# Weighted values of two attention groups: the bank summed by one VectorE reduction, the halves of v kept apart until the output projection

## The reference, cut to what matters

```python
weights = jnp.where(mask, jnp.exp(log_beta + later), 0.0)
return jnp.einsum('bhqk,bhkd->bhqd', weights.astype(v.dtype), v)
...
merged = jnp.concatenate([rmsnorm(merge_heads(o_sb), sb_out_norm),
                          rmsnorm(merge_heads(o_dl), dil_out_norm)], axis=-1)
return merged @ w_out
```

## Time and profile before

| | us |
|---|---|
| median of 3 runs (2080.09 to 2082.62) | 2080.28 |
| profiled execution | 2083.61 |
| its span | 2081.8 |

### The profile page before, as it was taken

How to read it: one execution, slowest core, us unless ns; L and a number is a source line. 1 busy time by engine, 2 the same in 40 slices (tenths; PEclk the granted TensorE clock), 3 DMA queues, 4 the chain that set the end, 5 groups by cost and what they waited for, 6 DMA issues and landing times. The chain is left out here.

```text
span 2081.8 us, 25977 instructions
## 1 busy us (share of the span) xinstructions
PE 1932.0 (93%) x9224; PEld 1582.6 (76%) x9224; DVE 1257.5 (60%) x1649; ACT 908.3 (44%) x1467; POOL 753.1 (36%) x506
## 2 busy tenths in 40 slices
PE   5899999999999898989989976896999999999998
PEld 4788888888888676767767755685788888888886
DVE  6855556555556266676676677327856556554555
ACT  6433333333335455555555555306433333333334
POOL 2656656530000252242242335304656556540000
PEclk9999999999999999999999986897999999999999
DMA  3443544558664310010101112511534435458663
GB/s 143 153 166 131 193 151 144 190 192 290 195 192 144 116 46 26 21 56 25 51 25 40 31 36 70 193 41 71 186 143 160 174 132 185 152 203 308 192 192 142
DMA packets 95584, 276.01 MB, mean 133 GB/s; under 512 B 10480, under 2 KB 14704, under 8 KB 89840
## 3 DMA queue, kind: packets, MB, share of 16 engines
q1 hardware_dynamic: 95472, 274.59, 38.7%
HBM read 190.14 MB, written 80.22 MB: 130 GB/s over the span
## 5 line engine op out<-in xcount | busy, mean ns | idle before, releaser
L703 PE MATMUL banks<-ffn_x_operands_hi 128*128 128x512 f32 x616 | 239.8, 389 | 0.0
L706 PE MATMUL banks<-ffn_x_operands_hi,ffn_x_operands_lo 128*128 128x512 f32 x616 | 239.7, 389 | 0.0
L705 PE MATMUL banks<-ffn_x_operands_lo,ffn_x_operands_hi 128*128 128x512 f32 x616 | 239.6, 389 | 0.0
L1265 DVE TENSOR_TENSOR heads_wt<-banks,heads_wt 128x512 fp32r<-128x512 f32 (+1 forms) x160 | 100.9, 632 | 134.7 <-ACT heads_wt L1109 133.9
L1382 PE MATMUL banks<-first_hi,w_hi 128*128 128x512 f32 x384 | 161.1, 420 | 13.5 <-ACT heads_qk_raw L1131 7.9
L401 ACT ACTIVATE scaled_rows<-banks 128x512 f32<-128x512 f32 x132 | 78.6, 595 | 201.9 <-PE banks L690 201.9
L516 DVE TENSOR_TENSOR scaled_rows<-banks,scaled_rows 128x512 f32<-128x512 f32 x132 | 91.1, 690 | 118.1 <-PE banks L690 74.4
L986 POOL TENSOR_TENSOR scaled_rows<-scaled_rows,heads_stay 128x128 f32<-128x128 f32 (+7 forms) x64 | 86.1, 1351 | 210.9 <-DVE heads_stay L1225 210.9
L1384 PE MATMUL banks<-first_hi,w_lo 128*128 128x512 f32 x384 | 152.2, 396 | 0.0
L1383 PE MATMUL banks<-first_lo,w_hi 128*128 128x512 f32 x384 | 152.0, 396 | 0.0
L687 PE MATMUL banks<-first_hi,ffn_w_ring_hi 128*128 128x512 f32 x352 | 139.1, 395 | 11.8 <-DVE first_lo L567 11.8
(11 more groups left out here) (183 smaller groups left out, 4821.0 us busy)
## 6 DMA issues: line engine op xcount, KB each, us to landing
w_raw<-in_ffn_w_gate SPq DMA_DIRECT2D x22, 1024.0 KB, 6.8
ffn_up_raw<-in_ffn_w_up SPq DMA_DIRECT2D x22, 1024.0 KB, 6.1
ffn_down_raw<-in_ffn_w_down SPq DMA_DIRECT2D x22, 1024.0 KB, 4.9
down_operands<-ffn_down_raw SPq DMA_DIRECT2D x22, 1024.0 KB, 7.3
w_raw<-h_operands SPq DMA_DIRECT2D x52, 256.0 KB, 3.0
ffn_up_raw<-h_operands SPq DMA_DIRECT2D x52, 256.0 KB, 3.0
ffn_down_raw<-h_operands SPq DMA_DIRECT2D x50, 256.0 KB, 3.0
w_raw<-in_w_in SPq DMA_DIRECT2D x24, 512.0 KB, 4.0
```

What stands on the lines that cost most here:

```text
L703: pe.matmul(out, hi[:, 0, tok], hi[:, 1, :], start=(opens and c == 0), stop=False, skip_group_check=True)
L705: pe.matmul(out, hi[:, 0, tok], lo[:, 1, :], start=False, stop=False, skip_group_check=True)
L706: last = pe.matmul(out, lo[:, 0, tok], hi[:, 1, :], start=False, stop=(c == NP - 1), skip_group_check=True)
L1265: dve.tensor_tensor(wt[:, wt_slot(s, j), 0:tiles, 1, :], b.ps[:, bank, 0:tiles * P].rearrange("p (t c) -> p t c", c=P), wt[:, wt_slot(s, j ...
```

## The change

ScalarE's copy and both VectorE adds are replaced by one VectorE reduction over the hi and lo columns of the bank, on all 128 partitions. `o_stage` and `o_dram` hold the two halves (products of v hi, products of v lo) apart. The wait of VectorE is now for `pv_ready`, TensorE's own. In the output block each piece is loaded as two, GpSimd adds them to `o_sum` (two tiles of `w_raw` and two new ones), ahead of each fold by two pieces; hi is taken from the first half, lo is the sum minus hi, and the squares are of the sum. The product of both lo parts is now part of the result.

```diff
-        o_stage = sb("o_stage", [HEAD, 2, SEQ])
+        o_stage = sb("o_stage", [P, 2, SEQ])
-        o_low = sb("o_low", [HEAD, 2, P])
...
             def store_part(it, kind, part):
                 cols = slice(part * HALF, (part + 1) * HALF)
                 sp.wait_ge(o_copied, 1 + STEPS * run(it, kind) + 4 * part + 4)
-                for head in range(2):
-                    first = address(sp, kind * GROUP + it * P + head * HEAD)
-                    sp.dma_start(o_dram[bass.ds(first, HEAD), cols], o_stage[:, head, cols]
-                                 ).then_inc(o_stored[part], 16)
+                first = address(sp, kind * GROUP + it * P)
+                for v_part in range(2):
+                    sp.dma_start(o_dram[v_part, bass.ds(first, P), cols].rearrange("(h r) c -> r h c", r=HEAD),
+                                 o_stage[v_part * HEAD:(v_part + 1) * HEAD, :, cols]).then_inc(o_stored[part], 16)
...
-            def values_low(it, kind, s):
-
-                act.wait_ge(pv_ready, 4 + BANKS * run(it, kind) + bank_count(s + 1))
-                act.activation(o_low[:, :, :], values[HEAD:P, :, 0, :], ACT.Copy
-                               ).then_inc(o_low_done, 1)
...
                     weights_hi(it, kind, s, j, project)
-                    if values_done(it, kind, s, j):
-                        values_low(*values_done(it, kind, s, j))
...
-                n = STEPS * run(it, kind) + s + 1
-                dve.wait_ge(o_low_done, n)
-                dve.tensor_tensor(o_low[:, :, :], values[0:HEAD, :, 1, :], o_low[:, :, :], ALU.add
-                                  ).then_inc(o_low_sum, 1)
-                dve.wait_ge(o_low_sum, n)
-                dve.tensor_tensor(o_stage[:, :, s * P:(s + 1) * P], values[0:HEAD, :, 0, :], o_low[:, :, :], ALU.add
-                                  ).then_inc(o_copied, 1)
+                dve.wait_ge(pv_ready, 4 + BANKS * run(it, kind) + bank_count(s + 1))
+                dve.tensor_reduce(o_stage[:, :, s * P:(s + 1) * P], values.rearrange("p a n c -> p a c n"),
+                                  mybir.AxisListType.X, ALU.add).then_inc(o_copied, 1)
...
+        o_more = sb("o_more", [P, 2, D])
+        o_sum = [part.rearrange("p (f c) -> p f c", c=OQ) for part in (
+            b.w_raw[:, 0, :, :].rearrange("p k f -> p (k f)"), b.w_raw[:, 1, :, :].rearrange("p k f -> p (k f)"),
+            o_more[:, 0, :], o_more[:, 1, :])]
...
-                    sp.dma_start(o_raw[n % 4], o_dram[group * GROUP:(group + 1) * GROUP, q * OQ:(q + 1) * OQ]
-                                 .rearrange("(f p) c -> p f c", p=P)).then_inc(o_loaded[n % 4], 16)
+                    for v_part, to in enumerate((o_raw, o_sum)):
+                        sp.dma_start(to[n % 4], o_dram[v_part, group * GROUP:(group + 1) * GROUP,
+                                                       q * OQ:(q + 1) * OQ]
+                                     .rearrange("(f p) c -> p f c", p=P)).then_inc(o_loaded[n % 4], 16)
...
+            def both_parts(n):
+                pool.wait_ge(o_loaded[n % 4], 32 * (n // 4 + 1))
+                pool.tensor_tensor(o_sum[n % 4], o_raw[n % 4], o_sum[n % 4], ALU.add).then_inc(o_added, 1)
+
+            for n in range(2):
+                both_parts(n)
             for n in range(2 * QUARTERS):
-
+                if n + 2 < 2 * QUARTERS:
+                    both_parts(n + 2)
                 first = n % 2 * (KT // 2)
                 pool.wait_ge(o_squared, n + 1)
...
-                    act.wait_ge(o_loaded[n % 4], 16 * (q // 2 + 1))
+                    act.wait_ge(o_loaded[n % 4], 32 * (q // 2 + 1))
...
-                    act.activation(o_sq[:, features(group), :], o_raw[n % 4], ACT.Square).then_inc(o_squared, 1)
+                    act.wait_ge(o_added, n + 1)
+                    act.activation(o_sq[:, features(group), :], o_sum[n % 4], ACT.Square).then_inc(o_squared, 1)
...
                     dve.wait_ge(o_hi_done, n + 1)
-                    dve.tensor_tensor(o_lo[:, features(group), tok], o_raw[n % 4],
+                    dve.wait_ge(o_added, n + 1)
+                    dve.tensor_tensor(o_lo[:, features(group), tok], o_sum[n % 4],
...
-    o_dram = nc.dram_tensor("o_between", [D, SEQ], F32, kind="Internal").ap()
+    o_dram = nc.dram_tensor("o_between", [2, D, SEQ], F32, kind="Internal").ap()
```

More of the change, by code:

```diff
@@ L863, in heads_block @@
         out_w_hi_done, out_w_gained, out_w_split = (sem(f"out_w_{n}") for n in ("hi_done", "gained", "split"))
-        pv_ready, o_low_done, o_low_sum, o_copied = (
-            sem("pv_ready"), sem("o_low_done"), sem("o_low_sum"), sem("o_copied"))
+        pv_ready, o_copied = sem("pv_ready"), sem("o_copied")
         o_stored = [sem(f"o_stored{h}") for h in range(2)]
@@ L1188, in step @@
                     split_out_weights(s)
-                if last and s == STEPS - 1:
-                    values_low(it, kind, s)
             def one_run(it, kind, first=0, end=STEPS, project=True, last=False):
@@ L1549, in output_block @@
         x_loaded = [sem(f"out_x_loaded{t}") for t in range(TT // 2)]
-        o_hi_done, o_split, o_squared = sem("out_o_hi_done"), sem("out_o_split"), sem("out_o_squared")
+        o_added, o_hi_done, o_split, o_squared = sem("out_o_added"), sem("out_o_hi_done"), sem("out_o_split"), sem("out_o_squared")
         o_halved, o_folded, stored = sem("out_o_halved"), sem("out_o_folded"), sem("out_x_stored")
```

## The result

The changed kernel took 2092.84 us in the median of 4 runs (2092.66 to 2094.54), beside 2081.28 us (2080.09 to 2082.62, 4 runs) for the kernel before on the same chip: a ratio of 1.0052, with a 95% interval of 1.004 to 1.0064. Between the medians it is slower by 11.6 us in the first set and by 9.4 in the second; the forecast was 2082.1, with a range up to 2091.

A forecast was written before the change was run, and what follows sets the result against it. TensorE was taken as the bound, busy 1932.0 of 2081.8 us, so only its waits count. Heads -7.8, stores 0, output block +9.6 gave +1.8 us on the 2080.28 median: 2082.1 us, range 2074 to 2091.

The forecast's parts named there:

- The signs: What would show the forecast: reduction near 0.69 us, copy-out waits 4 to 5 us smaller, heads about 8 us shorter.
- The first step, 26 waits x 0.17: Heads: TensorE's 26 waits for the copy out of the values' bank each end 0.17 us earlier, 4.4 us.
- the sum of the three, 7.8 us of waits: Heads: 4.4 us from named waits, 2.2 from half the other 27, 1.2 in the last run; 7.8 us less.
- third rival: Heads: shorter waits save a third of the lost clock, 6.3 us, on top; 2075.8 us; chance 0.19.
- 9.6 forecast: Output block: the fifth bank starts 9.6 us later, through later loads and GpSimd's adds and folds before the sums.
- From there TensorE is full, so the 9.6 us stay: Output block behind the second sums: TensorE is full, so the 9.6 us delay stays.
- GpSimd's chain to the second sums ends later still and hides that: Output block: a slower clock after the 5 us stall doubles the third bank's 2.7 us, but GpSimd's chain hides it.
- The adds at 2.0 us: Output block: each GpSimd add of the two halves takes 2.0 us.
- Stores at zero, up to +1: Heads' end: only the last, larger store counts; taken as zero, with ends -0.4 and +1 us.
- the 0.6 us "earlier": Heads' end: the last store starts 0.6 us earlier through the lost ScalarE copy and the 0.17, offsetting its later landing.
- The first rival: Output block loses 13 us with adds at 2.4 us, heads gain only 4.4; 2088.9 us; chance 0.26.
- its smaller gain in the heads: First rival's heads: only the 26 named waits shorten, 4.4 us.

The follow-up runs named there:

- the second: Later set timing the same changed kernel again, against the kernel before: 2091.46 us, ratio 1.0046 (1.0032 to 1.006).
- without adds: Changed kernel with double loads but GpSimd's adds left out, hi, lo and squares from the first half: 2078.37 us, 0.9984 to the kernel before.
- Heads alone: Changed heads with the kernel before's output block, which reads only the first half: 2075.28 us, 0.9965 to the kernel before.
- the two kernels built on it: Changed heads, old output block: with ScalarE's copy put back, 2075.67 us; with one reduction for each head instead of one for both, 2080.44 us.
- adds behind folds: Changed kernel with GpSimd's queue reordered, both folds of a quarter before the next adds: 2084.61 us, 1.001 to the kernel before.
- with the adds on VectorE: Changed kernel with the adds of the halves moved from GpSimd's queue to VectorE's: 2081.04 us, 0.9992 to the kernel before.
- with x loaded later: Changed kernel with the adds on VectorE and the first load of x issued behind both groups' loads: 2082.46 us, 0.9998 to the kernel before.

## Why the prediction was wrong

**Where it held.** The reduction took 0.68 us (forecast 0.69); the place in the queue 0.60. Here the rule of the Trainium skill ("VectorE: DVE Perf Modes") can be judged: by its section on the perf-mode tier table a reduction runs at the single rate, and the trace agrees, since 512 numbers take as long as in the two-input subtraction (680 and 686 ns). The advice of its Rules for kernel authors, to restructure a reduction as the slowest op, isn't borne out where two dependent adds are what it replaces. The heads won 7.5 us (forecast 7.8), the copy 1 to 2 of them (forecast 1.2). TensorE's first matmul came 2.95 us later (forecast 2.6), and it stood before both sums, for the folds, in the order worked out. Mechanism and sign of both parts were right.

**Where the heads were right by luck.** The signs asked for TensorE's waits for the copy out 4 to 5 us smaller; they are 2 to 3 us smaller (33.6 to 33.7 in three profiles of the old one, 30.4 to 31.9 in seven of the new). The first step, 26 waits x 0.17, was too large, and so was the sum of the three, 7.8 us of waits: TensorE's idle time fell by about 3 us in all. That a shortened step ends at the next wait would explain it, and is not shown. The other 4.4 us are busy time, at a higher granted clock. That is the third rival's mechanism, with less than its 6.3 us and not on top of the forecast. That shorter waits raised the clock is the reading of two numbers side by side; no run here separates it.

**Where it failed: the terms of the output block**, 9.6 forecast and 14.9 us in this profile. The path was right; its pieces were sized too small, and the clock and the store were put at nothing. By the table of marks, in the order of their size in this profile:

- *"From there TensorE is full, so the 9.6 us stay"*: 1.7 us more came behind the second sums. TensorE was full, but not fast: the clock fell at 1333.86, after the 1.9 us stall. With the folds first, or without adds, that stretch took 80.8 us as before.
- *"GpSimd's chain to the second sums ends later still and hides that"*: it doesn't, 1.4 us. The chain begins with ScalarE's root of the first sums, and the sums themselves ran at the lower clock, 1.86 us instead of 0.95. So the squares came 3.96 us after the sums' start where I had taken 3.04 from the row before, and everything behind them is later by 0.9; the rest is the add (2.35 us until the fold behind it, for 2.0) and some 0.2 us before and in the fold ahead of it. Cover can't be claimed for a chain that starts from the slowed instruction.
- *The adds at 2.0 us*: 2.35 to 2.40 us. One stands ahead of the first lo part. Up to the first sums only the third and the fourth count in the queue, as the earlier ones wait for loads. Together with a third load that landed 9.5 us after the first instead of 8.7, fold 1 ended 18.3 us after the first landing; 17.1 had been worked out. That is 1.2 us, 0.35 of them before the first matmul. In the other two profiles of this block the third load came 10.8 and 10.9 us after the first, and this term is the largest of the four, at 2.5 us and more. Part of it was in the rows: the earlier trace rows give one landing for the fifth and the sixth load, 1319, but the sixth landed at 1319.9, which makes 3.1 us a MB instead of 2.9.
- *Stores at zero, up to +1*: 0.97 us, at the upper end. The two stores land 3.2 us after issue instead of 2.3, and the 0.6 us "earlier" that I set against it is not found here: measured from the end of the last copy out, it lies in the heads' gain, and I had set it against the stores as well. Heads alone and the two kernels built on it show the same within 0.02 us.

0.97 + 1.2 + 1.4 + 1.7 = 5.3 us, and 9.6 + 5.3 = 14.9. With the heads at -8.8 that makes +6.1 us; the other 2.6 us of this profile lie in blocks that the change doesn't touch. Against the medians one more thing counts: the profiled execution of before was itself 3.3 us above the 2080.28 from which the forecast was counted (2.3 above the median of all four runs), that of after at its median.

**The range.** The first rival was nearest: adds at 2.4 us, 13 us lost in the output block, 2088.9 us. Its price for the block was 2 us short of this profile, for the clock and the store, where it shared the forecast's terms (worked through again with its own 2.4 and 2.6 us, the block's loss is 12.4 us rather than 13), and its smaller gain in the heads didn't come. The range reached 2091 by its adds and the smaller gain. The ends of terms that I had named myself are 3.4 us for the adds, 1 for the store, and the slower clock, which I had put at nothing and which cost 2.6 (0.9 ahead of the second sums, 1.7 behind them): all of them raise the same stage, and came together. With them in one sum the block alone leads to 2082.1 + 7.0 = 2089.1 us, and the smaller gain in the heads on top, 3.4, to 2092.5. The measured 2092.84 lies just above even that.

## What to carry to other kernels

Taking work off the chain of one stage by handing its remainder to the next is a price paid where the next stage starts cold: there nothing hides an operation. Before an in-order queue gets a new instruction that waits for a transfer, list what stands behind it; here the order alone was worth 8 us and the choice of engine 10 to 12, more than the whole gain that was sought. When a stall on TensorE is forecast, add the slower clock to everything that starts from TensorE's next instruction, and once more after the next stall. A term that hangs on queued loads is better taken from several profiles: here one landing, against the first, moved by 1.4 us between profiles of the same block.

## What the hardware showed beyond that

- A VectorE reduction over pairs 512 bytes apart in a PSUM bank costs what it reads: 680 ns for 512 numbers a partition, 414 for 256. The distance costs nothing that shows.
- The same add of 128x1024 float32 numbers in SBUF took 1.23 us on VectorE and 2.35 to 2.40 us on GpSimd; GpSimd's product of the same shape took 2.00 us. Shape and type alone didn't tell its time within a fifth.
- A VectorE subtraction that takes 1.22 us took 2.22 when GpSimd folded beside it (adds behind folds, VectorE's timeline below), and the fold of 128x256 under it 1.59 us instead of 0.74. The subtraction ran from 1307.79 to 1310.01, across the end of one fold (1308.92) and the start of the next (1309.00 to 1310.59), as if each got at the memory only once the other was done; that is a reading of these times, not shown. So work moved from one of the two engines to the other isn't free for either.

```profile
1307.79 2.22 DVE L1640 TENSOR_TENSOR out_o_lo<-w_raw,out_o_hi 128x1024 fp32r<-128x1024 f32 x1 [4.15 <-POOL w_raw L1586]
```

- A stall of 1.9 us, which began 3 us after TensorE had got its full clock back, was followed by a second spell at 1.2 GHz. In the kernel without adds TensorE stood 1.6 us for a bank at 1316.7 and 0.3 us for the second sums, and the clock stayed at 1.00 from 1320 to 1350. A long stall just before isn't needed for it: with the adds on VectorE TensorE stood 1.86 us before the first sums and the clock was low from 1316.4 to 1319.8; with x loaded later it stood 1.00 us there and the clock stayed up.
